# A hybrid decoder step: convolution tiles set into the item loop of the attention

## The reference

```
hc, gc, gb, cq, ckv, kpe = split(rms(h) @ w_in)          # 3 x 512, 384, 256, 32 columns
up = concat([conv_prev, gc * hc]); y_conv = gb * (w0*up[t] + w1*up[t+1] + w2*up[t+2])
ckv = rms(ckv); kpe = rope(kpe); q = rms(cq) @ w_uq      # 8 heads, 64 + 32 wide
q_lat = q_nope @ w_uk                                    # queries in latent space
prompt: causal softmax((q k) * scale) v, per head, blocks of 128 queries
sample: softmax over 2048 cached rows of pool[page_table] and the 4 new ones, in latent space
h = h + concat([y_conv, y_att]) @ w_out
```

## Time and profile before

| | us |
|---|---|
| median of 3 runs | 1545.83 |
| lowest and highest | 1545.02, 1547.13 |
| span of the profiled execution, first to last instruction | 1544.0 |
| TensorE busy in it | 1487.7 |
| VectorE busy | 1013.7 |
| mean granted TensorE clock | 0.981 |

### The profile page before, as it was taken

How to read it: one execution, slowest core, us unless ns; L and a number is a source line. 1 busy time by engine, 2 the same in 40 slices (tenths; PEclk the granted TensorE clock), 3 DMA queues, 4 the chain that set the end, 5 groups by cost and what they waited for, 6 DMA issues and landing times.

```text
span 1544.0 us, 18899 instructions
## 1 busy us (share of the span) xinstructions
PE 1487.7 (96%) x7084; PEld 1194.0 (77%) x7084; DVE 1013.7 (66%) x2038; ACT 269.8 (17%) x566; POOL 102.7 (7%) x114
## 2 busy tenths in 40 slices
PE   8999989799999999999999899999999999999996
PEld 6887645478888888888877778788888888888875
DVE  3363354568776676766774876877866766767845
ACT  4000034322101101001132321022001011011223
POOL 0012212500000000000100000400000000000100
PEclk9999988799999999999999999999999999999998
DMA  8305667622222222222213121122222222222201
GB/s 323 114 23 156 197 182 212 192 93 82 82 82 82 82 82 83 82 82 82 97 55 133 63 82 55 58 83 82 82 83 82 82 83 82 83 82 96 83 28 58
DMA packets 39469, 152.36 MB, mean 99 GB/s; under 512 B 6673, under 2 KB 19378, under 8 KB 26706
## 3 DMA queue, kind: packets, MB, share of 16 engines
q1 hardware_dynamic: 34258, 134.37, 25.0%
q0 software_dynamic: 5120, 16.78, 3.7%
HBM read 148.11 MB, written 3.02 MB: 98 GB/s over the span
## 4 chain that ended last, share of the span: by engine, by line
PE 91%; DVE 5%; another core or an unknown queue 2%; issue 1%; ACT 0%; DMA 0%; DVEq 0%; SPq 0%; ACTq 0%
PE psum L531 68%; PE psum L501 14%; PE psum L773 1%; PE psum L667 1%; PE psum L486 1%; PE psum L702 1%; PE psum L794 1%; PE psum L730 1%; PE psum L782 0%; PE psum L595 0%; PE psum L738 0%; DVE small L1553 0%; PE psum L652 0%; PE psum L835 0%
## 5 line engine op out<-in xcount | busy, mean ns | idle before, releaser
L531 PE MATMUL psum<-arena 128*128 128x272 f32 x2016 | 479.2, 393 | 0.0
L531 PEld LDWEIGHTS psum<-arena 128*128 128x128 f32 x2016 | 383.0, 190 | 78.7
L1161 DVE TENSOR_TENSOR arena<-psum,arena 128x272 f32<-128x272 f32 x564 | 248.7, 441 | 248.1 <-PE psum L531 225.1
L531 PE MATMUL psum<-B,ring 128*128 128x272 f32 x736 | 184.7, 393 | 4.1 <-ACT B L881 1.9
L501 PE MATMUL psum<-A,ring 128*128 128x272 f32 x672 | 161.0, 401 | 8.1 <-DMA ring<-in_weights 7.1
L531 PE MATMUL psum<-arena,ring 128*128 128x272 f32 x672 | 167.7, 392 | 0.0
L531 PEld LDWEIGHTS psum<-B,ring 128*128 128x128 f32 x736 | 139.0, 190 | 33.5 <-issue 2.5
L501 PEld LDWEIGHTS psum<-A,ring 128*128 128x128 f32 x672 | 129.8, 194 | 38.0 <-ACT A L1003 7.1
L531 PE MATMUL psum<-A,ring 128*128 128x272 f32 x608 | 152.6, 393 | 1.6 <-DVE A L1613 1.5
L531 PEld LDWEIGHTS psum<-arena,ring 128*128 128x128 f32 x672 | 127.4, 190 | 26.0
L531 PEld LDWEIGHTS psum<-A,ring 128*128 128x128 f32 x608 | 115.4, 190 | 26.0 <-DVE A L1613 2.0
(11 more groups left out here) (228 smaller groups left out, 1274.6 us busy)
## 6 DMA issues: line engine op xcount, KB each, us to landing
ring<-in_weights SPq DMA_DIRECT2D x98, 1024.0 KB, 4.8
arena<-in_keys SPq DMA_DIRECT2D x128, 144.0 KB
arena<-in_attw SPq DMA_DIRECT2D x1, 3072.0 KB, 21.0
h<-in_xT SPq DMA_DIRECT2D x4, 544.0 KB, 7.7
out_yT<-A SPq DMA_DIRECT2D x8, 272.0 KB, 2.3
arena<-in_pemb SPq DMA_DIRECT2D x2, 544.0 KB, 5.8
ring<-in_weights SPq DMA_DIRECT2D x2, 512.0 KB, 6.5
arena<-in_bias SPq DMA_DIRECT2D x1, 640.0 KB, 8.2
```

Source lines behind the costliest of these rows:

```text
L531: end = pe.matmul(bank(g, n), lhs[:, c, :], x(c), start=c == 0, stop=c == 3)
L1161: ins = dve.tensor_tensor(out, bank(g, n), more, ALU.add)
```

## The change

The nine tiles `in_ab(9)` to `in_ab(17)` (nine of the twelve of the convolution) are no longer computed ahead of the loop; tile 9 + i follows item 3i (`CONV_AT`), in one PSUM slot of its own, and `conv` is cut into four parts that VectorE takes in the items of `CONV_STEPS`. The key and value tiles come right behind the query latents, with score pairs 0 and 1. Everything else of the sample's attention goes into the loop: pairs 2 to 7 in items 0 to 5, the softmax of group 0 in items 7 to 11, its values with the scores of group 1 in items 12 to 19, group 1's softmax in items 21 to 25 and its values in items 25 to 32.

Buffers move for it: `K` lies in `h`, so x is loaded a second time once the keys have been used; value rows have three buffers in place of six; weight units 6, 7 and 8 go to ring places 0, 1, 0, and `AFTER` names the unit whose tiles each has to wait for. Turned probabilities of an item have one bank in place of two, and so have the outputs. SP's list and GpSimd's are written anew. The first halves of four products of output group 0 are computed in items 32, 33 and right behind them.

The diff, cut to its core:

```diff
-T_COL = [0, 1, 3, 4, 5, 6, 7, 10, 11, 21, 22, 23, 24, 25, 26, 27, 28, 29]
 T_NQ, T_NKV = 8, 9
 T_UQ = 12
 T_QL = T_UQ + 8
-T_UK = 30
+T_UK = T_QL + 1
 T_UV = T_UK + 4
-T_OUTAB = T_UV + 4
+T_CONV = T_UV + 4
+T_COL = [0, 1, 3, 4, 5, 6, 7, 10, 11] + [T_CONV + i for i in range(9)]
+T_OUTAB = T_CONV + 9
...
+CONV_AT = {3 * i: 9 + i for i in range(9)}
+CONV_STEPS = {0: {0: 0, 1: 1, 2: 2, 3: 3}, 1: {8: 0, 9: 1, 11: 2, 12: 3}, 2: {17: 0, 18: 1, 20: 2, 22: 3},
+              3: {26: 0, 27: 1, 28: 2, 29: 3}}
+STEP_AT = {n: (c, part) for c, steps in CONV_STEPS.items() for n, part in steps.items()}
...
+RING_OF = {6: 0, 7: 1, 8: 0}
+AFTER = {4: 0, 5: 1, 6: 4, 7: 5, 8: 6, 9: 7, 12: 8}
...
-        vring = arena[:, 4352:8448].rearrange("p (s b n) -> p s b n", s=2, b=4)
+        vring = arena[:, 4352:6400].rearrange("p (b n) -> p b n", b=4)
...
-        A_flat = A[:, :, :].rearrange("p k t -> p (k t)")
-        K = A_flat[:, 0:4096].rearrange("p (h n) -> p h n", h=H)
+        h_flat = h[:, :, :].rearrange("p k t -> p (k t)")
+        K = h_flat[:, 0:4096].rearrange("p (h n) -> p h n", h=H)
...
-        v_slot = lambda s: s % 8 if s % 8 < 6 else s % 2
-        v_use = lambda s: (0 if s < 6 else 1 if s < 8 else 2 if s < 10 else 1 if s < 14 else 3)
-        v_buf = lambda i: vring[:, i, :, :] if i < 2 else ring[:, (i - 1) % SLOTS, :].rearrange("p (b n) -> p b n", b=4)
+        v_slot = lambda s: s % 3
+        v_use = lambda s: s // 3
+        v_buf = lambda i: vring if i == 0 else ring[:, 1 + i, :].rearrange("p (b n) -> p b n", b=4)
...
+                if u in AFTER:
+                    sp.wait_ge(psum_full, tiles_through(AFTER[u]))
+                elif u >= SLOTS and u >= U_OUTAB + 4:
                     if group_of(u - SLOTS) is not None:
                         sp.wait_ge(prod, done(group_of(u - SLOTS), P4))
                     else:
                         sp.wait_ge(psum_full, tiles_through(u - SLOTS))
-                sp.dma_start(ring[:, u % SLOTS, :], a["weights"][u]).then_inc(w_loaded[u % SLOTS], 16)
+                sp.dma_start(ring[:, ring_of(u), :], a["weights"][u]).then_inc(w_loaded[u % SLOTS], 16)
...
+            def x_again(i):
+                sp.dma_start(h[:, 2 * i:2 * i + 2, :], xT[:, 2 * i:2 * i + 2, :]).then_inc(x_loaded[i], 16)
+
             for m in range(2):
                 keys(m)
-            for u in range(4, 9):
-                unit(u)
-            for m in range(2, 10):
-                keys(m)
+            unit(4)
+            unit(5)
             sp.wait_ge(dve_x, 4)
             sp.dma_start(a["ckvT"].rearrange("(k p) t -> p k t", p=P), ckv).then_inc(stored, 16)
+            sp.wait_ge(qs_ready, 1)
+            sp.dma_start(a["kpeT"], ssum[64:96, :]).then_inc(stored, 16)
+            for m in range(2, 4):
+                keys(m)
+            unit(6)
+            for m in range(4, 10):
+                keys(m)
+            unit(7)
+            keys(10)
+            unit(8)
+            for m in range(11, 16):
+                keys(m)
+            unit(U_OUTAB)
+            sp.wait_ge(sc_full, 24)
+            x_again(0)
+            x_again(1)
+            unit(U_OUTAB + 3)
             sp.wait_ge(conv_done, 1)
-            sp.dma_start(a["kpeT"], ssum[64:96, :]).then_inc(stored, 16)
             sp.dma_start(a["convp"].rearrange("p c t -> p (c t)"), ctails[:, 0:8]).then_inc(stored, 16)
             sp.dma_start(a["convs"].rearrange("p c b t -> p (c b t)"), ctails[:, 8:72]).then_inc(stored, 16)
-            for m in range(10, 16):
-                keys(m)
-            for u in range(U_OUTAB, U_OUTAB + 4):
-                sp.wait_ge(v_used, u - U_OUTAB + 11)
+            for u in (U_OUTAB + 1, U_OUTAB + 2):
+                sp.wait_ge(v_used, u - U_OUTAB + 13)
                 unit(u)
+            sp.wait_ge(sc_full, NPR)
+            x_again(2)
+            x_again(3)
...
+            for s, tiles in ((1, T_COL[5] + 1), (2, T_COL[7] + 1), (0, T_UQ + 8)):
+                pool.wait_ge(psum_full, tiles)
+                gather(s)
+            for s in range(3, 16):
+                pool.wait_ge(v_used, s - 2)
+                gather(s)
...
-            in_ab(9)
-            in_ab(10)
-            pe.wait_ge(ql_ready, 2)
-            for m in range(7):
-                in_ab(11 + m)
-                score_pair(m)
-            score_pair(7)
-            score_new(0)
...
+                if i == 1:
+                    pe.wait_ge(ql_ready, 1)
+                    score_pair(0)
+            score_pair(1)
 
             def paged(n):
 
-                if n < 16:
-                    if n % 2 == 0:
-                        values_pair(0, n // 2)
-                    else:
-                        score_pair(8 + n // 2)
-                elif n == 16:
+                if n < 6:
+                    score_pair(2 + n)
+                elif n == 6:
+                    pe.wait_ge(ql_ready, 2)
+                    score_new(0)
+                elif n == 9:
+                    turn(0, 0)
+                    turn(0, 1)
+                elif n == 10:
+                    turn(0, 2)
+                    turn(0, 3)
+                elif n == 11:
+                    turn(0, 4)
+                elif 12 <= n < 20:
+                    values_pair(0, n - 12)
+                    score_pair(n - 4)
+                elif n == 20:
                     values_new(0)
                     score_new(1)
-                elif n == 17:
+                elif n == 21:
                     turn_out(0)
-                elif n < 23:
-                    if n == 19:
-                        pe.wait_ge(ol_ready, 1)
-                    turn(1, n - 18)
-                elif 24 <= n < 32:
-                    values_pair(1, n - 24)
+                elif n == 23:
+                    turn(1, 0)
+                    pe.wait_ge(ol_ready, 1)
+                    turn(1, 1)
+                elif n == 24:
+                    turn(1, 2)
+                    turn(1, 3)
+                elif n == 25:
+                    turn(1, 4)
+                    values_pair(1, 0)
+                elif 26 <= n < 32:
+                    values_pair(1, n - 25)
                 elif n == 32:
+                    values_pair(1, 7)
                     values_new(1)
                 elif n == 33:
                     turn_out(1)
...
+            def out_first(product_n, cs):
+
+                lhs, x, c_sem, x_at = {P1: (quarter(U_OUTAB, 0, 0), lambda c: B[:, 2 * c, N1], None, None),
+                                       P3: (wsum(0, 4), lambda c: B[:, 2 * c + 1, N2], None, None),
+                                       P2: (quarter(U_OUTAB, 0, 1), lambda c: B[:, 2 * c + 1, N1], None, None),
+                                       P6: (wsum(0, 2), lambda c: XT_AB(1, c), xt_ready, lambda c: c + 1)}[product_n]
+                product(0, product_n, lhs, x, c_sem, x_at, cs)
...
-                    if m >= 2:
-                        pe.wait_ge(pt_ready, m - 1)
+                    if m >= 1:
+                        pe.wait_ge(pt_ready, m)
                     for j in range(i + 1):
-                        last = pe.transpose(psum[:, 2 + m % 2, j * P:(j + 1) * P],
+                        last = pe.transpose(psum[:, 7, j * P:(j + 1) * P],
                                             Pp[:, m % 2, j * P:(j + 1) * P], ident[:])
                     last.then_inc(pt_full, 1)
                 paged(n)
+                if n in CONV_AT:
+                    in_ab(CONV_AT[n])
+                if n == 32:
+                    pe.wait_ge(w_loaded[U_OUTAB % SLOTS], 16 * (U_OUTAB // SLOTS + 1))
+                    pe.wait_ge(conv_done, 1)
+                    pe.wait_ge(pexp, 31)
+                    out_first(P1, range(2))
+                elif n == 33:
+                    pe.wait_ge(wsum_ready, 1)
+                    pe.wait_ge(pexp, 32)
+                    out_first(P3, range(2))
                 if n >= 2 and m % 2:
                     q = m // 2
                     pe.wait_ge(pt_ready, m + 1)
-                    if q >= 2:
-                        pe.wait_ge(y_free, q - 1)
+                    if q >= 1:
+                        pe.wait_ge(y_free, q)
                     for j in range(i + 1):
                         for odd in range(2):
                             v_cols = slice((hd - 1 + odd) * VD, (hd + odd) * VD)
-                            last = pe.matmul(psum[64 * odd:64 * odd + 64, 6 + q % 2, 0:P], vtok[:, j, v_cols],
+                            last = pe.matmul(psum[64 * odd:64 * odd + 64, 6, 0:P], vtok[:, j, v_cols],
                                              PTp[:, odd, j * P:(j + 1) * P], start=j == 0, stop=j == i)
                     last.then_inc(y_full, 1)
+            pe.wait_ge(psum_free, T_OUTAB)
+            out_first(P2, range(2))
+            out_first(P6, range(2))
...
+                    if g == G_OUTAB:
+                        dve.wait_ge(x_loaded[j], 32)
...
+                if n in (2, 4, 6):
```

(41 more changed lines are left out.)

149 lines of the change are left out of this document (78 added, 71 removed).

## The result

The changed kernel takes **1566.36 us** (median of 4 runs, 1564.33 to 1571.84) against 1546.48 for the kernel before, run beside it: a ratio of 1.0131, 95% interval 1.0107 to 1.0155. It is 19.9 us slower. The prediction said slower, by 4.9 (1551, range 1537 to 1564).

The account below looks back on a forecast made before the run. TensorE, busy for 96% of the span, was taken to bound the kernel. Losses of 2 + 11.5 + 6 + 7 + 18 = 44.5 us against 39.6 to win made it 4.9 slower: 1551 us, range 1537 to 1564.

Parts of the forecast that it names:

- term 1: Behind the query latents, key and value tiles meet a low clock: 2 us lost, items begin at 128.5.
- term 2: First items: score pairs 2 and 4 wait for keys, the latter behind unit(6), then slow clock: 11.5 us, bounds 6 and 13.
- term 3: Items 7 to 11 and 20 to 25: each item's softmax chain leaves TensorE idle, 6 us, bounds 2 and 9.
- term 4: Items 12 to 19: key waits exposed at pairs 11 and 14, some lower clock: 7 us, bounds 2 and 16.
- term 5: Last eight value pairs, items 25 to 32: GpSimd's gather issue sets the pace, 18 us lost, bounds 13 and 23.
- The clock stays up: Rival: a tile every third item keeps TensorE at 2.4 GHz through the loop; 33 lost, 1539 us, chance 0.26.
- Signals come promptly: Rival: TensorE's signals are not delayed by gathers; terms 4 and 5 fall by 5 together, 1546 us, chance 0.18.
- Gathers hold everything: Rival: gathers and value pairs' signals wait on each other; terms 4 and 5 reach 16 and 23, 1565 us, chance 0.08.

Follow-up runs that it names:

- keys_ahead: The changed kernel with the keys of pairs 4, 5 and 6 issued ahead of unit(6) in SP's queue: 1557.1 us, ratio 1.0149 to the kernel before.
- pairs_apart: The changed kernel with score pairs 2 to 7 in items 0, 1, 3, 4, 6, 7, keys 4 and 5 ahead of unit(6), softmax later: 1563.9 us, ratio 1.0107.
- unit8_late: The changed kernel with unit(8), the last two projection tiles' weights, behind the keys of pair 13 instead of pair 10: 1559.4 us, ratio 1.018.
- before_again: The kernel before, unchanged, run once more for its trace: 1546.7 us.
- after_again: The changed kernel, unchanged, run once more beside the kernel before on one chip: 1566.1 us, ratio 1.0144.
- before_no_keys: The kernel before without the key transfers of pairs 2 to 15, all gathers kept: 1543.2 us.
- before_no_gathers: The kernel before without the gathers of value pairs 6 to 15: 1521.7 us.
- before_direct: The kernel before with the value rows of pairs 6 to 15 fetched by SP's direct transfers instead of GpSimd's gathers: 1546.2 us, ratio 0.9979.
- tiles_keys_split: The changed kernel with tiles moved toward later items, keys 4 to 6 ahead of unit(6), value rows of pairs 11 to 15 half by SP: 1555.4 us, ratio 1.0028.
- all_moves: As tiles_keys_split, but score pairs 2 to 7 spread as in pairs_apart, tiles at 11 and 13, last turned row behind item 11's tile: 1552.7 us, ratio 1.0013.
- no_gathers: The changed kernel without the gathers of value pairs 3 to 15: 1540.1 us.

## Why the prediction was right in direction and wrong in size

*Start (term 1)*: item 0's first score came at 128.96 for 128.5.

*Keys for pairs 2 and 4 (term 2)*: the waits were 1.70 and 6.90 for 2 and 6.5, at half clock behind the second as said. Item 0 to the first value pair took 71.9 against 59.9 without keys: 12.0 for 11.5. The size was right. Its cause was right in part only: with `unit(6)` out of the way the wait moved to pair 5 and fell to 3.60, and what then held was the ring of two pairs (`keys_ahead`). The clock was luck besides: the wait before pair 2 cost none here, and 3.3 us in `keys_ahead` and `pairs_apart`.

*Chain (term 3)*: the idle times of items 7 to 11 were 0.58, 1.35, 0.36 and 1.16, and stayed the same without transfers; those of items 20 to 25 came to some 2 without transfers. 5.5 for 6.

*Items 12 to 19 (term 4)*: **the step that failed.** It had 7, bounds 2 and 16. Value pair 0 to value pair 8 took 96.8, and 79.2 without transfers: 17.6. The waits at items 15 and 18 were the ones named (3.45, 3.57 for 2 to 3). In the windows above the 17.6 are 10.4 more of idle time, 7.0 of it these two waits, and 7.2 more of busy time for the same matmuls, where the term had 1 to 3 for the lower clock. The slow clock came three times (8.26, 9.22 and, in item 21, 8.79 for a tile of 7.53), not once. What was missed is that keys and rows cost more together than apart: 8 us for gathers alone, 1.7 for keys alone, 17 for both. The term had held transfers of 7.5 us an item against work of 6.6 and let prefetched buffers cover the rest, and had then costed two exposed latencies one by one. That the shared rate is what couples the two is argued from a DMA share of 0.89 over 200.81 to 265.23 and 1.06 at its height; no run varies the rate by itself. The same loss puts value pair 8 at 297.6 instead of 288.

*Last eight value pairs (term 5)*: GpSimd's five gathers took 27.7 us, 298.94 to 326.7, for 25, with one gap of 2.47; from the end of value pair 8 to the projection it took 41.3 (298.6 to 339.9) where 20.1 + 18 were expected: 21 lost, inside the bounds of 13 to 23. A third of it, though, is no transfer: without any, the same stretch still takes 27.2 (269.8 to an equal start at 297.0), 7 more than the work, part of it the waits for VectorE's copies above.

The predicted 44.5 thus became 1.3 + 12.0 + 5.5 + 17.6 + 21.2 = 57.6; the stretch itself (110.95 to 339.9, less 173.1 of work) gives 55.8. The terms overlap by the 1.8 between these. Of the 15.7 us between forecast and result, some 11 are term 4 by itself and 3 are term 5; the rest is the scatter at either end, less that overlap.

*Rivals.* "The clock stays up" fell: 0.70, 0.86, 0.84 and 0.69 in the windows above. The page "TensorE: Matmul & The Clock Gate" of the Trainium skill (section "What's actually happening"), which has activity release the clock, agrees with these rows, where it fell behind waits; what failed was the hope that a tile in every third item leaves no such wait. "Signals come promptly" turned out to be a matter of the chip and not of the difference: on one where none was late, the last stage was some 5 us shorter, as the rival had it, but the kernel before was faster too, and `keys_ahead` and `unit8_late` stood at 1.015 and 1.018. "Gathers hold everything" gave terms 4 and 5 as 16 and 23 and the time as 1565, nearly what came, and I had it at 0.08; its mechanism is only half of it, since without keys the middle stage loses 8 us to gathers and not 16.

Of the 39.6 us that the kernel before loses, 25 to 29 go with its gathers and 3 to 6 with its keys. The forecast rested on the thought that the new order exposes the gathers more. It doesn't: it exposes the keys, whose loads had stood under dense tiles (0.98 clock) and now stand between short items.

## What to carry to other kernels

Before spreading dense work over a loop, list for each transfer the work that lies between its signal and its use: before, a tile of 7.5 us stood ahead of each of the pairs 0 to 6; after, two tiles stand among pairs 2 to 7. Leaving a kind of transfer out of both kernels, and then both kinds, costs six runs and puts the difference where it belongs; comparing only the changed kernel with and without gathers (26 us) would have blamed the wrong one. Where two streams run together and the DMA share is near 1, cost the two together, and not each latency.

## What the runs showed of the hardware

*Late signals belong to GpSimd's gathers and to the chip.* The first fence is the waits of the changed kernel in 200 to 345 (engine and line, what it waited for, total us, times, longest); "remote" is a signal that came well after its instruction's recorded end. The second is the same view of `keys_ahead`, with the same gathers, on another chip, where no "remote" is listed:

```profile
ACT arena L1160 <- remote: 20.0, 5, 5.9
DVE psum L1659 <- remote: 17.7, 4, 7.0
PE psum L709 <- DMA arena<-in_keys: 7.0, 2, 3.6
POOL ring L468 <- remote: 5.2, 3, 2.5
```
```profile
PE psum L711 <- DMA arena<-in_keys: 10.2, 2, 6.0
PEld psum L746 <- DMA ring<-in_rows,vidx: 7.4, 2, 4.0
```

Both kernels' first runs, `before_again`, `after_again` and `before_no_keys` have them; `before_no_gathers` and `before_direct`, on chips where the kernel before took 1550.3, have none behind 213. On the chip of `before_no_gathers`, `tiles_keys_split` and `all_moves`, which gather, have them; and in `before_direct` itself ScalarE gets pair 7's signal at 194.41, 3.4 us after its end, behind an early gather (188.52 to 193.2), while no signal is late after 213, where SP fetches. So gathers are needed, and a chip on which they act so. The 0.07 us of the Trainium skill's page "TensorE: Matmul & The Clock Gate" (section "The cost: per-tile semaphore tail") agrees with `before_no_gathers`, where no semaphore update of TensorE came over 0.05 us behind its recorded end in that stretch, and with `keys_ahead`, whose gathers ran on the chip without late signals (0.05 us at most there too). It does not agree with the runs that have them. The kernel before ran in 1534.9 on the chip without late signals and in 1546.8 to 1550.3 on the others; that late signals are the reason is likely and was not shown, since no trace of the kernel before comes from that chip.

*Short waits can cost the clock.* A wait of 1.83 us in `pairs_apart` was followed by 12.4 us of half or mixed clock (2.79 and 9.63, for 1.43 and 7.53), one of 1.70 at the same place in the changed kernel by none (1.50 and 7.60), and one of the same 1.70 there in `no_gathers` by 2.77 and 9.67 again. So the length of the wait alone does not decide. What does stays open. TensorE's timeline of `no_gathers`:

```profile
130.94 2.77 PE L706 MATMUL psum<-arena 96*32 96x256 f32 x24 [1.70 <-DMA arena<-in_keys]
133.64 9.67 PE L540 MATMUL psum<-A,ring 128*128 128x272 f32 x32
```
